# Opening on one queue with gains multiplied out of PSUM, and a recurrence layer that projects its conv branch first

## The reference, cut to what matters

```python
gate_br, x_br = jnp.split(xn @ w_in, 2, axis=-1)        # two halves of 1024 columns
x_br, new_buf = causal_dwconv(x_br, conv_buf, conv_w, conv_b)   # 4 taps over time
r = sigmoid(einsum(xb, w_a) + b_a);  i = sigmoid(einsum(xb, w_x) + b_x)   # 8 blocks of 128
log_a = -LRU_C * r * softplus(-lam);  a = exp(log_a)
u = sqrt(-expm1(2.0 * log_a)) * (i * x_br)
h = a_t * h + u_t                                       # scan over time, from state_lru
y = gelu(gate_br) * hs;  out = y @ w_out
```

## Time and profile before

| | us |
|---|---|
| timed runs, median (lowest to highest) | 1956.38 (1956.15 to 1957.5) |
| profiled execution, its own time | 1956.49 |
| its span, first to last instruction | 1954.9 |
| PE busy | 1774.0 |
| VectorE busy | 1324.6 |
| ACT busy | 950.4 |
| POOL busy | 498.7 |
| mean granted TensorE clock over the span | 0.948 |

### The profile page before, as it was taken

How to read it: one execution, slowest core, us unless ns; L and a number is a source line. 1 busy time by engine, 2 the same in 40 slices (tenths; PEclk the granted TensorE clock), 3 DMA queues, 4 the chain that set the end, 5 groups by cost and what they waited for, 6 DMA issues and landing times.

```text
span 1954.9 us, 35706 instructions
## 1 busy us (share of the span) xinstructions
PE 1774.0 (91%) x13457; PEld 1644.5 (84%) x13457; DVE 1324.6 (68%) x2471; ACT 950.4 (49%) x1722; POOL 498.7 (26%) x419
## 2 busy tenths in 40 slices
PE   6999989999999365899999959999999998999998
PEld 6998759999999233599999959999899875999997
DVE  5989795555575877465557876554799879565455
ACT  4456754453344755255435454533545666445333
POOL 1601401441120334154112015411160060044111
PEclk8999989999999667899999979999999998999999
DMA  6455474655547899765554517554545448465550
GB/s 211 142 181 152 141 230 133 201 183 183 172 169 233 314 398 410 266 207 186 173 172 135 170 55 234 178 183 161 157 139 184 125 137 265 130 200 177 183 175 26
DMA packets 317972, 365.05 MB, mean 187 GB/s; under 512 B 7802, under 2 KB 290978, under 8 KB 317750
## 3 DMA queue, kind: packets, MB, share of 16 engines
q1 hardware_dynamic: 296068, 287.41, 46.7%
q0 software_dynamic: 20560, 74.62, 10.1%
q10 hardware_dynamic: 1216, 1.35, 0.2%
HBM read 340.79 MB, written 23.15 MB: 186 GB/s over the span
## 4 chain that ended last, share of the span: by engine, by line
PE 66%; DVE 18%; ACT 7%; issue 3%; DVEq 3%; DMA 1%; POOLq 1%; POOL 0%; ACTq 0%; SPq 0%
PE G L551 19%; PE G L552 19%; PE G L553 19%; DVE wlo L1681 5%; ACT whi L1061 3%; DVE sums L1994 2%; PE A L997 1%; PE A L512 1%; DVE pg L2056 1%; DVE pg L2054 1%; DVE xbc L1842 1%; ACT raw L1247 1%; PE G L748 1%; DVEq L1844 1%; DVE stx L1986 1%
## 5 line engine op out<-in xcount | busy, mean ns | idle before, releaser
L1681 DVE TENSOR_TENSOR wlo<-raw,whi 128x2048 fp32r<-128x2048 f32 x234 | 547.7, 2341 | 335.8 <-ACT whi L1061 335.6
L1061 ACT ACTIVATE whi<-raw 128x2048 fp32r<-128x2048 f32 x234 | 448.0, 1914 | 560.0 <-PE G L553 555.8
L551 PE MATMUL G<-xH,whi 128*128 128x264 f32 x2112 | 605.0, 286 | 16.9 <-DVE wlo L1681 12.3
L552 PE MATMUL G<-xH,wlo 128*128 128x264 f32 x2112 | 600.1, 284 | 0.0
L553 PE MATMUL G<-xL,whi 128*128 128x264 f32 x2112 | 599.8, 284 | 0.0
L551 PEld LDWEIGHTS G<-xH,whi 128*128 128x128 f32 x2112 | 399.5, 189 | 26.8 <-DVE wlo L1681 13.5
L552 PEld LDWEIGHTS G<-xH,wlo 128*128 128x128 f32 x2112 | 399.7, 189 | 0.1
L553 PEld LDWEIGHTS G<-xL,whi 128*128 128x128 f32 x2112 | 397.8, 188 | 0.0
L551 PE MATMUL G<-aH,whi 128*128 128x264 f32 x1024 | 292.2, 285 | 7.9 <-DVE wlo L1681 7.9
L553 PE MATMUL G<-aL,whi 128*128 128x264 f32 x1024 | 290.7, 284 | 0.0
L552 PE MATMUL G<-aH,wlo 128*128 128x264 f32 x1024 | 290.7, 284 | 0.0
(11 more groups left out here) (440 smaller groups left out, 3032.2 us busy)
## 6 DMA issues: line engine op xcount, KB each, us to landing
raw<-in_mlp_w_up SPq DMA_DIRECT2D x64, 1024.0 KB, 5.3
raw<-in_mlp_w_down SPq DMA_DIRECT2D x64, 1024.0 KB, 5.1
raw<-in_ssd_w_in SPq DMA_DIRECT2D x48, 1024.0 KB, 5.4
pg<-in_cache_k POOLq DMA_DIRECT2D x64, 512.0 KB, 7.3
raw<-in_ssd_w_out SPq DMA_DIRECT2D x16, 1024.0 KB, 6.8
raw<-in_ple_w_gate SPq DMA_DIRECT2D x16, 1024.0 KB, 5.1
raw<-in_moba_w_qkv SPq DMA_DIRECT2D x12, 1024.0 KB, 5.2
pgw<-in_cache_v POOLq DMA_DIRECT2D x24, 512.0 KB, 7.4
```

Source lines behind the costliest of these rows:

```text
L551: mm(o, whi[u % 2][:, k, w], act_h[:, x, :], start=first, stop=False)
L552: mm(o, wlo[u % 2][:, k, w], act_h[:, x, :], start=False, stop=False)
L1061: fn(whi[u % 2][:], raw[(u + 2) % 4][:], ACT.Copy).then_inc(s_hi, 1)
L1681: V.tensor_tensor(wlo[u % 2][:], raw[(u + 2) % 4][:], whi[u % 2][:].bitcast(F32), ALU.subtract).then_inc(s_lo, 1)
```

## The change

Opening: SP requests the inputs in two halves (`s_x`) and goes on to the weight chunks at once. ACT's queue keeps the samples and the gain rows; the twelve factor loads go to POOL's queue. PE transposes the gain rows first, then each half as it lands, and adds three 512-column matmuls whose output is not used. DVE multiplies the gains by bank straight out of PSUM into `xg`, and ACT copies `h`. ACT runs one root ahead of all, and four squares into separate buffers, which DVE adds; POOL has no part in it. The factor rows are transposed behind chunk 0 (`factor_rows`).

Recurrence layer: the chunk order is 4 to 7, then 0 to 3. The states are requested at layer 1's gate stage, transposed behind chunk 0, copied by ACT and pre-multiplied by POOL, which makes the sample columns of `xc` too (`s_lpool`). All gates run within the projection, behind chunks 2 to 5. Gelu is one ACT step in place. DVE's and ACT's sequences are written out in a new order, and the last product and `oH`, `oL` go in a half and two quarters. Three semaphores are shared with others instead of being their own. Core of the diff:

```diff
 SP
-            sp.wait_ge(s_load, 16 * 6)
+            for c in range(2):
+                sp.dma_start(A0["xrow"][:, c, :], t_in["x_prompt"][0][c * P:(c + 1) * P, :]).then_inc(s_x[c], 16)
...
-                    loads(stage[i, "lru_in"])
+                    for r in range(8):
+                        load_one(stage[i, "lru_in"], r, (r + 4) % 8)
 PE
+            pe.wait_ge(s_load, 16 * 5)
+            tr(bank[3][:, 0:104], A0["rowA"][:], 104).then_inc(s_tp0, 1)
             for c in range(2):
+                pe.wait_ge(s_x[c], 16)
                 for k in range(KT):
                     t_ = tr(G[c][:, k // 4, ...], A0["xrow"][:, c, k * P:(k + 1) * P], P)
+                    if k % 4 == 3:
+                        t_.then_inc(s_tp0, 1)
...
+            for k in range(3):
+                mm(bank[1], ident[:], A0["xrow"][:, 0, 0:512], start=True, stop=True)
...
+                    if q == 0 and is_first(it) and u == 0:
+                        factor_rows()
                     if is_first(it) and u == 1:
+                        pe.wait_ge(s_ev, 1)
...
                 def after_in(it, u):
+                    r = it * 4 + u
+                    if r == 0:
+                        states()
+                    if 2 <= r < 6:
+                        gates(2 * r - 4)
+                        gates(2 * r - 3)
+                project(stage[2, "lru_in"], xH, xL, norm=6, after=after_in, peel=True)
 ACT, opening
+            act.wait_ge(s_const, 1)
+            fn(rstd[:, 0:1], epsc[:, 0:1], ACT.Sqrt)
             act.wait_ge(s_raw[0], 16)
             fn(whi[0][:], raw[0][:], ACT.Copy).then_inc(s_hi, 1)
+            act.wait_ge(s_h, 1)
+            fn(h[:, :, 0:P], G[0][:]..., ACT.Copy)
             for r in range(4):
                 high(0, r)
+            fn(h[:, :, P:SEQ], G[1][:]..., ACT.Copy)
+            fn(h[:, :, SEQ:T], bank[0]..., ACT.Copy).then_inc(s_h, 1)
             act.wait_ge(s_raw[1], 16)
             fn(whi[1][:], raw[1][:], ACT.Copy).then_inc(s_hi, 1)
+            act.wait_ge(s_h, 3)
+            for u, o in enumerate((ssq, hh2, Z["xbc"][:, 0:2, :], Z["xbc"][:, 2:4, :])):
+                fn(o, h[:, 2 * u:2 * u + 2, :], ACT.Square).then_inc(s_sq, 1)
 ACT, recurrence layer
+                for u in range(4):
                     split(st, 0, u); (u == 0: root(6))
+                    first_tap(u)
+                    (u == 0: copies lstT, lh0; u > 1: two gate_tanh)
+                split(st, 1, 0)
+                decay(0)
+                gate_tanh(4); gate_tanh(5)
+                split(st, 1, 1)
+                one_decay(0)
+                gate_tanh(6); gate_tanh(7)
+                split(st, 1, 2)
+                decay(1)
+                one_decay(1)
+                root_of(0); root_of(1)
+                for u in range(4):
+                    gelu(u)
+                for n in range(3):
+                    out_high(n)
+                split(st, 1, 3)
 POOL
+                pool.wait_ge(s_lTe, 1)
+                for k in range(3):
+                    gp.tensor_tensor(lpr[:, :, :, k], ..., by_channel(k * KT, KT), ALU.mult)
+                (two adds, then one add into lspre, each behind a drain)
+                for u in range(4):
+                    pool.wait_ge(s_ev, c0 + u + 1)
+                    gp.tensor_tensor(xc[:, pair, SEQ:T], XR[:, pair, 3 + SEQ:3 + T], by_channel(3 * KT + 2 * u, 2), ALU.mult)
+                    pool.drain()
+                    gp.tensor_tensor(xc[:, pair, SEQ:T], xc[:, pair, SEQ:T], lspre[:, pair, :], ALU.add).then_inc(s_lpool, 1)
+            def lru_loads():
+                pool.wait_ge(s_mm, stage[1, "gate"]["g0"])
 DVE, opening
+            for c in range(2):
+                for k in range(KT):
+                    (k % 4 == 0: wait for that bank)
+                    f = V.tensor_scalar(xg[:, k, c * P:(c + 1) * P], G[c][:, k // 4, ...], colA[:, k:k + 1], None, ALU.mult)
+            V.tensor_tensor(xg[:, :, SEQ:T], bank[0]..., colA..., ALU.mult).then_inc(s_xg, 4)
             (wlo[0]; low(0, r); wlo[1])
+            V.tensor_tensor(ssq, ssq, hh2, ALU.add)
+            V.tensor_tensor(sq2, sq2, sq3, ALU.add)
+            V.tensor_tensor(ssq, ssq, sq2, ALU.add).then_inc(s_ssq, 1)
             (colB, colC, colE)
 DVE, recurrence layer
+                split(st, 0, 0); rms(6); evicted(0); conv(0)
+                for r in range(1, 4):
+                    evicted(r); split(st, 0, r); conv(r)
+                log_a(0)
+                evicted(4); split(st, 1, 0); one_less_square(0)
+                evicted(5); split(st, 1, 1); log_a(1)
+                evicted(6); split(st, 1, 2); one_less_square(1)
+                scan(0)
+                evicted(7)
+                gated(halves[0])
+                scan(1)
+                gated(slice(4, 6)); gated(slice(6, 8))
+                for k in (0, 2, 4, 6):
+                    out_low(k, max(0, k // 2 - 1))
+                split(st, 1, 3)
```

More of the change, by code:

```diff
@@ L278, in build_trunk @@
                                                  sem("s_pje"), sem("s_tg"))
-        s_fin, s_finT, s_finE = sem("s_fin"), sem("s_finT"), sem("s_finE")
+        s_fin, s_finE = sem("s_fin"), sem("s_finE")
+        s_x, s_h = [sem(f"s_x{c}") for c in range(2)], sem("s_h")
         s_mtp, s_msc, s_mex, s_mP = sem("s_mtp"), sem("s_msc"), sem("s_mex"), sem("s_mP")
@@ L372, in sum_adds @@
         def sum_adds(m):
-            return 3 * m
+            return 3 * (m - 1)
         def split_input(n):
@@ L931, in lru, with states @@
             def lru():
-                def states(it, u):
-                    if not (is_first(it) and u == 3):
-                        return
+                def states():
                     pe.wait_ge(s_lld, 16 * 4)
@@ L1358, in gate_tanh, with first_tap, gelu, decay @@
                     fn(L["thi"][:, k, :], A[k % 2][:, 1, 0:T], ACT.Tanh, scale=0.5, bias=lsp["bxh"][:, k:k + 1]).then_inc(s_lth, 1)
+                halves = (slice(0, 4), slice(4, 8))
+                def first_tap(u):
+                    act.wait_ge(s_ev, st["c0"] + u + 1)
+                    for k in (2 * u, 2 * u + 1):
+                        fn(xc[:, k, 0:SEQ], XR[:, k, 0:SEQ], ACT.Identity, bias=colB[:, 32 + k:33 + k], scale=colB[:, k:k + 1]).then_inc(s_lt0, 1)
+                def gelu(u):
+                    act.wait_ge(s_ev, st["c0"] + 4 + u + 1)
+                    pair = L["Gt"][:, 2 * u:2 * u + 2, :]
+                    fn(pair, pair, ACT.Gelu_apprx_tanh).then_inc(s_lgt, 1)
+                def decay(n):
+                    act.wait_ge(s_lla, n + 1)
+                    fn(thr[:, halves[n]], la[:, halves[n]], ACT.Tanh, scale=-1.0)
+                    fn(L["a2"][:, halves[n]], la[:, halves[n]], ACT.Exp, scale=2.0).then_inc(s_la, 1)
+                def one_decay(n):
+                    fn(la[:, halves[n]], la[:, halves[n]], ACT.Exp).then_inc(s_lb, 1)
+                def root_of(n):
+                    act.wait_ge(s_lv, n + 1)
+                    fn(thr[:, halves[n]], thr[:, halves[n]], ACT.Sqrt).then_inc(s_lsq, 1)
+                def out_high(n):
+                    act.wait_ge(s_ly, n + 1)
+                    part = (slice(0, 4), slice(4, 6), slice(6, 8))[n]
+                    fn(lo_["oH"][:, part], xc[:, part], ACT.Copy).then_inc(s_mixh, 1)
                 for u in range(4):
@@ L2235, in lru @@
-                for u in range(4):
-                    split(st, 0, u)
-                    if u == 0:
-                        rms(6)
-                        V.memset(L["XR"][:, :, 0:3], 0.0)
-                    dve.wait_ge(s_mm, st["g0"] + u + 1)
-                    V.tensor_tensor(Gt[:, 2 * u:2 * u + 2, :], G[(u + st["c0"]) % 2][:, :, 0:T], bc(rstd[:], 2), ALU.mult).then_inc(s_ev, 1)
-                    dve.drain()
-                    gelu_in(u)
-                    if u:
-                        gelu_out(u - 1)
@@ L2246, in lru, with conv @@
-                halves = (slice(0, 4), slice(4, 8))
-                thr, thi, hs = L["thr"], L["thi"], L["hs"]
+                XR, xc, la, Gt = L["XR"], L["xc"], L["la"], L["Gt"]
+                thr, thi, hs = L["thr"], L["thi"], L["hs"]
+                halves = (slice(0, 4), slice(4, 8))
+                def conv(u):
+                    dve.wait_ge(s_lt0, 2 * u + 2)
+                    for w in range(1, CW):
+                        for k in (2 * u, 2 * u + 1):
+                            f = V.scalar_tensor_tensor(xc[:, k, 0:SEQ], XR[:, k, w:w + SEQ], colB[:, w * KT + k:w * KT + k + 1], xc[:, k, 0:SEQ], ALU.mult, ALU.add)
+                            if w == CW - 1:
+                                f.then_inc(s_lc, 1)
+                        if w < CW - 1:
+                            dve.drain()
```

254 lines of the change are left out of this document (111 added, 143 removed).

## The result

The changed kernel took **1939.03 us** (median of 4 runs, 1935.98 to 1940.03) against 1956.27 for the kernel before beside it (1955.35 to 1957.5): a ratio of 0.9903, 95% interval 0.989 to 0.9917. The forecast was 1937.0, its range 1929 to 1946. The profiled execution took 1939.22 us with a span of 1937.6.

The account below looks back on a forecast made before the run. PE is busy 91% of the span, so only stretches where it stands still or runs at its lower clock can give much. 1956.5 less 7.7 (opening) and 12 (recurrence layer) gives 1937 us, range 1929 to 1946.

Parts of the forecast that it names:

- Recurrence layer, forecast 12: Recurrence layer: conv half first puts gates, decay and scan beside gate chunks; PE resumes 12.6 us earlier, net 12, bounds 8 to 16.
- The 0.7 us set aside for POOL: Recurrence layer: allowance for PE's first gate waiting on POOL's sample conv; nothing to 16.5 us held possible, 0.7 taken.
- Opening, forecast 7.7: Opening: loads no longer wait for gain rows, so chunk 1 starts at 22.4 instead of 30.14, 7.7 us; bounds 4 to 9.
- the forecast's lower bound of 4: Opening: only 4 us gained if gain rows come as late as before, the chunk runs cold, or factors are late.
- now only 32 KB stand before them: Opening: gain rows, behind only 32 KB on their queue, take 3 us and land near 5.9.
- (a): Rival: VectorE's lack of slack costs the recurrence layer 3 us, opening keeps 4 to 5: 1944; chance 0.19 together with (d).
- (b): Rival: split and table load end beside other work (16), opening gives 9: 1931; chance 0.11 for below 1932.
- (c): Rival: late POOL sample rows stop PE's gates, 1953 or 1963; chance 0.04 between 1952.5 and 1960.4, 0.04 above.
- (d): Rival: chunk 1 waits for late factor rows until 30, recurrence gain alone remains, 1944.5; chance 0.19 together with (a).

Follow-up runs that it names:

- decay first: Changed kernel with ACT's second-half decay ahead of the weight split, and VectorE's one_less_square(1) ahead of that chunk's eviction: 1933.78 us, ratio 0.9877.

## Why the prediction was right, and which terms were off

*Recurrence layer, forecast 12, measured 12.6.* Step by step as laid out. The forecast put the first root at 1123.2, 53.3 behind the layer's start of the earlier trace rows's trace (1069.88); it came 53.1 behind it. PE's restart on `oL` was forecast at 65.3 behind it, and measured at 65.31; the stop 13.6, and 13.7. The restart cost what it did: the first output chunk took 7.5 us to ACT's next split (1131.54 to 1139.02), 7.8 before. Gelu took 0.63 to 0.64 for a pair (three of them 1.71), by tanh 0.6, and nothing waited for it. The 0.7 us set aside for POOL was not paid: its small instructions took 0.22 to 0.60 where the bound from the earlier trace rows had a quarter of 2.71, and the two that met a `wlo` took 2.2 but nobody waited.

*Opening, forecast 7.7, measured 4.7.* At the second chunk the seven profiles with the changed opening stand at 25.37 on average, the two with the old at 29.81, a gain of 4.4; at the mark 147.96 and 152.67, 4.7. The gain lasted, as forecast. That 4.7 + 12.6 = 17.3 is just what the span lost is partly luck: in that one profile the mark came 4.1 earlier, layer 2 only 3.7, and 1.0 more was gained behind the output projection's start. So is the nearness of the total: the forecast took 19.5 off, and the changed kernel came out 17.2 below before one time and 21.9 the other. It is the size that was off, in this step: "now only 32 KB stand before them ... I take 3, so they land near 5.9". They landed at 8.23, hardly sooner than before (8.41): of the three things behind the forecast's lower bound of 4, the "gain rows as late as before" came true. The step looked only at the gain rows' own queue; issued ahead of all else they are in use 1.6 us later, beside the other queue's megabytes 5.4. The old trace also had rows against the 3 and against the 9.1 as the slowest: a load of 8 KB took 5.0, and one of 512 KB 12.4.

```profile
pg<-in_cache_v POOLq DMA_DIRECT2D x8, 512.0 KB, 12.4
prow<-in_p_sample POOLq DMA_DIRECT2D x4, 8.0 KB, 5.0
```

Two smaller misses follow: 0.26 instead of 0.2 for a multiply of 128 columns (16 in 4.23), and 10.41 instead of 8.0 for the first weight chunk. The last was hidden, until the gain rows were put first; there the weight chunk came at 11.94, and that alone was enough to leave the first chunk where it was. So the step that failed would not have given all its time even if its landing had been right (with the weight chunk at 10.41 the first chunk would have come near 15.4 by that run, an estimate, where 13.5 was forecast): two transfers were mis-sized, and the later of them sets the start.

*The rivals.* (a) did not happen: no chunk of the layer waited for a `wlo` (its 1944 should read 1942.5 to 1943.5: 9 for the layer, 4 to 5 for the opening). (b) did not happen in the changed kernel, and decay first is not quite its case: split and table load stay on the chain there, and it is the decay that leaves it, for 2.2 us at the restart where (b) counted 3.2. (c) was refuted by POOL's rows, (d) by the chain: the factor rows' transposes began at 24.68, right behind the norm's matmuls. The root began 0.01 after its table load of 1.28 ended (1118.29 against 1118.28). The Trainium skill's drain of some 1.38 beside each load (ScalarE: Activation LUTs, What ACT_TABLE_LOAD costs) shows in no trace here.

## What to carry to other kernels

A layer laid out instruction by instruction from durations of the old trace came out to a few tenths; a transfer's landing did not: the same four loads took 5.4 us in one order and 1.6 in another. Ask what the other queues move at the time, and which transfer is last after the one that is moved. When a stop remains, look at the in-order engine that was idle just before it: here 3.2 us of ACT's idle time ahead of a split, and a consumer that could have begun with half of its input, were worth 1.3 and 4.0 us more at the end of the first output chunk. Measure such a gain behind the restart, not at it: 0.9 of the first one's 2.2 was lost there. Compare stages by their own lengths; starts late in a long program carry the variation of everything before, and a spell seen in one profile may be missing in the next of the same kernel.

## What was not expected of the hardware

- Four small loads took 5.4 us from the last issue to their first use while another queue had megabytes to move, and 1.6 us when issued ahead of it (on that queue).
- The 900 us from layer 0 to layer 2 varied by 7.6 us among twelve profiles with next to no edit in them, while a layer of 65.3 us repeated to 0.03.
- A first chunk that began at the lower level (0.71 to the second chunk) cost 0.7 to 2.0 us at the second chunk, and nothing that shows at the mark 120 us later.
- The same three matmuls took 2.84 us in four profiles and 4.58 to 5.09 in five, at a granted clock that reads 1.00 in both.
- A POOL instruction of 16 columns took 0.22 us alone and 2.2 beside a VectorE `wlo`.
